# Experts' tokens gathered for two pairs at once in split products of 256 columns, the scatter moved to the pairs between, and the spare weight buffer removed

## What is computed

```python
# hier_moe: 32 experts in 4 groups of 8, top 2 within the chosen group
g_logits = h @ w_grp + b_grp; grp = argmax(g_logits)
top_val, top_idx = lax.top_k(e_logits of that group, 2)
gate = softmax(top_val) * p_grp
for each expert e, on its tokens xb:
    out = (silu(xb @ w1[e]) * (xb @ w3[e])) @ w2[e]
y = sum over a token's two experts of gate * out
x = x + g2 * y
```

## Time and profile before

| what | value |
|---|---|
| runs of the kernel before | 1750.25, 1750.30, 1751.11 us, median 1750.3 |
| profiled execution, its own time | 1750.12 us |
| its span | 1748.3 us |
| outside the span | 1.8 us |
| TensorE busy, share of the span | 99% |
| granted TensorE clock, mean | 0.998 |
| DMA, mean of the program | 244 GB/s |
| experts, first issue of a load to the end | 1258.2 to 1748.3 us |

### The profile page before, as it was taken

How to read it: one execution, slowest core, us unless ns; L and a number is a source line. 1 busy time by engine, 2 the same in 40 slices (tenths; PEclk the granted TensorE clock), 3 DMA queues, 4 the chain that set the end, 5 groups by cost and what they waited for, 6 DMA issues and landing times.

```text
span 1748.3 us, 30291 instructions
## 1 busy us (share of the span) xinstructions
PE 1729.7 (99%) x12581; PEld 1415.8 (81%) x12582; DVE 908.9 (52%) x1570; ACT 701.2 (40%) x1179; POOL 166.2 (10%) x173
## 2 busy tenths in 40 slices
PE   9999999999999999999999999999999999999998
PEld 8999988999999999998899999677774445444443
DVE  6655577676655766567678666466731111111111
ACT  6444545464344543454445445454631111111111
POOL 1000042210000100014214000100410000000000
PEclk9999999999999999999999999999999999999999
DMA  9545464545444445557556455232199999999997
GB/s 381 198 173 182 156 250 168 208 169 172 178 181 169 169 173 180 179 169 241 194 192 226 172 192 189 89 85 73 75 421 405 429 427 428 428 428 430 427 428 312
DMA packets 78815, 425.89 MB, mean 244 GB/s; under 512 B 16352, under 2 KB 32992, under 8 KB 41824
## 3 DMA queue, kind: packets, MB, share of 16 engines
q1 hardware_dynamic: 78256, 421.01, 62.7%
q10 hardware_dynamic: 432, 3.10, 0.4%
HBM read 423.03 MB, written 1.05 MB: 243 GB/s over the span
## 4 chain that ended last, share of the span: by engine, by line
PE 90%; DMA 6%; ACT 2%; DVE 2%; issue 1%; POOL 0%; POOLq 0%; SPq 0%; DVEq 0%; ACTq 0%
PE ps L721 18%; PE ps L723 18%; PE ps L722 18%; PE ps L1373 10%; PE ps L1424 5%; DMA ring<-stream_expert 5%; PE ps L1347 3%; PE ps L1049 2%; PE ps L1043 2%; PE ps L1055 2%; PE ps L815 1%; PE ps L1354 1%; ACT w_split L1486 1%; PE ps L1355 1%; DVE w_split L1939 1%
## 5 line engine op out<-in xcount | busy, mean ns | idle before, releaser
L1939 DVE TENSOR_TENSOR w_split<-ring,w_split 128x1024 fp32r<-128x1024 f32 x335 | 425.0, 1276 | 334.1 <-ACT w_split L1486 333.5
L721 PE MATMUL ps<-x_hi,w_split 128*128 128x272 f32 (+1 forms) x1856 | 541.1, 292 | 2.1 <-DVE x_lo L1944 1.7
L723 PE MATMUL ps<-x_hi,w_split 128*128 128x272 f32 (+1 forms) x1856 | 534.0, 288 | 0.0
L722 PE MATMUL ps<-x_lo,w_split 128*128 128x272 f32 (+1 forms) x1856 | 532.1, 287 | 0.0
L1486 ACT ACTIVATE w_split<-ring 128x1024 fp32r<-128x1024 f32 x335 | 350.6, 1054 | 354.4 <-PE ps L723 353.2
L721 PEld LDWEIGHTS ps<-x_hi,w_split 128*128 128x128 f32 x1856 | 350.4, 189 | 14.6 <-issue 9.6
L722 PEld LDWEIGHTS ps<-x_lo,w_split 128*128 128x128 f32 x1856 | 350.4, 189 | 0.3
L723 PEld LDWEIGHTS ps<-x_hi,w_split 128*128 128x128 f32 x1856 | 350.3, 189 | 0.0
L723 PE MATMUL ps<-hid_hi,w_split 128*128 128x272 f32 (+1 forms) x704 | 201.6, 286 | 0.0
L722 PE MATMUL ps<-hid_lo,w_split 128*128 128x272 f32 (+1 forms) x704 | 201.5, 286 | 0.0
L721 PE MATMUL ps<-hid_hi,w_split 128*128 128x272 f32 (+1 forms) x704 | 201.1, 286 | 0.0
(11 more groups left out here) (427 smaller groups left out, 2212.5 us busy)
## 6 DMA issues: line engine op xcount, KB each, us to landing
ring<-stream_ffn SPq DMA_DIRECT2D x131, 1024.0 KB, 4.8
ring<-stream_expert SPq DMA_DIRECT2D x48, 2048.0 KB, 25.0
ring<-stream_expert SPq DMA_DIRECT2D x36, 1024.0 KB, 12.8
arena<-stream_expert SPq DMA_DIRECT2D x16, 2048.0 KB, 25.5
ring<-stream_in SPq DMA_DIRECT2D x27, 1024.0 KB, 4.9
ring<-stream_mod SPq DMA_DIRECT2D x24, 1024.0 KB, 6.9
con<-stream_expert SPq DMA_DIRECT2D x8, 2048.0 KB, 26.1
ring<-stream_out SPq DMA_DIRECT2D x12, 1024.0 KB, 4.9
```

The lines of the kernel that those rows point to most:

```text
L721: pe.matmul(to, w[:, 0, k], hi, start=first, stop=False)
L722: pe.matmul(to, w[:, 0, k], lo, start=False, stop=False)
L723: return pe.matmul(to, w[:, 1, k], hi, start=False, stop=last_)
L1939: nc.vector.tensor_tensor(w[:, 1], half_of(n), w[:, 0].bitcast(fp32), ALU.subtract).then_inc(split_ready, 1)
```

## The change

- **Gather.** After pair 0 tokens are no longer gathered for each pair. In pairs 1, 3, ... 13 (`own == 1`) TensorE gathers the tokens of the next two pairs at once (`gather_two`): 256 columns, and the transposed features split into a high and a low float32r part (`h2t_hi`, `h2t_lo`), 32 products in all: 16 between gate and up, 8 on each side of the four transposes. Pairs 0 and 1 are still gathered one by one in float32 (`gather_one`). The selection `sel` becomes float32r and twice as wide.
- **Split.** In pair 0 ScalarE copies `h2t` to `h2t_hi` (two of 128x1024) and VectorE subtracts (two of 128x1024) into `h2t_lo`, which lies over `h2t`.
- **Scatter.** In pairs 2, 4, ... 14 the scatter of the pair before is done after up, four blocks on each side of the four transposes; in the other pairs up to 13 it stays between gate and up. In pair 15 nothing moves.
- **Tokens.** `xs` now holds two pairs' tokens in three pieces (`token_chunks`). The scaling is of 256 columns, four blocks on ScalarE and four on VectorE in every second pair. `e_hid` is gone: the product goes into `e_act` in place. `sel_gate` moves to the table memory.
- **No spare.** The memory of the spare is now `h2t_hi` and the last tokens (the tensor `vec` grows by 512 columns). `place_of` is gone: half q of unit m goes to the place of unit m-9, and waits for exactly that half (`again`). `whole` waits for the second half of unit m-9.
- **Loop.** Two iterations of six pairs in place of four of three, on TensorE, ScalarE and VectorE. SyncE's loop is as before.

```diff
-            for (unit, q), freed in zip(units(RING_SLOTS, 2 * RING_SLOTS), [None] + units(0, RING_SLOTS)):
...
-                    if freed is not None:
-                        sp.wait_ge(big_done, pass_ * PASS_DONE + big_used(*freed))
...
+                for unit, q in units(RING_SLOTS, 2 * RING_SLOTS):
+                    again(pass_, 0, unit, q)
                 for unit in range(2 * RING_SLOTS):
...
-                    whole(pass_, 1, unit, unit >= RING_SLOTS)
+                    whole(pass_, 1, unit)
```

```diff
+            def gather_two(n, bank, first):
+
+                pe.wait_ge(sel_ready, n + 3)
+                for c in (first, first + 1):
+                    to = ps[:, bank, (c % 2) * SEQ:(c % 2) * SEQ + SEQ]
                     for t in range(2):
...
+                        pe.matmul(to, h2t_hi[:, t, c * P:c * P + P], sel[:, t], start=t == 0, stop=False)
+                        last = pe.matmul(to, h2t_lo[:, t, c * P:c * P + P], sel[:, t], start=False, stop=t == 1)
                 last.then_inc(gathered, 1)
```

```diff
+                first = isinstance(i, int) and i == 0 and u == 0
+                two = own == 1 and more_pairs
...
+                gate_or_up(pass_, i, u, 0, halves, own)
+                if first or two:
+                    pe.wait_ge(selT_ready, n + 1)
+                    pe.wait_ge(ye_ready, 2 * n + 2)
+                    scatters(range(C))
+                if two:
+                    if isinstance(i, int) and i == 0 and isinstance(pass_, int):
+                        pe.wait_ge(split_ready, H2_DONE)
+                    gather_two(n, 6, 0)
+                    gather_two(n, 7, 2)
+                gate_or_up(pass_, i, u, 1, halves, own)
+                if first:
+                    gather_one(n + 1, 0, 1, tokens_of(pass_))
+                elif two:
+                    pe.wait_ge(xs_ready, n + 2)
+                    gather_two(n, 6, 4)
                 else:
...
+                    pe.wait_ge(ye_ready, 2 * n + 2)
+                    scatters(range(C // 2))
                 pe.wait_ge(e_hid_ready, n + 1)
```

```diff
+                if own == 1 and more_pairs:
+                    act.wait_ge(big_done, n * (2 * BIG_SLOTS) + 6)
+                    gathered_two(n, 0)
+                    gathered_two(n, 1)
+                if first:
+                    if split:
+                        for t in range(2):
+                            last = nc.scalar.activation(h2t_hi[:, t], h2t[:, t], ACT.Copy)
+                        last.then_inc(hi_ready, 1)
+                    gathered_one(n + 1, 1)
```

More of the change, by code:

```diff
@@ L646, in again, with whole @@
                 big(i * TURN + u, u, b, q)
-            def whole(pass_, i, unit, wait):
-                if wait:
-                    sp.wait_ge(big_done, pass_ * PASS_DONE + i * TURN_DONE + big_used(unit - RING_SLOTS, 1))
+            def whole(pass_, i, unit):
+                sp.wait_ge(big_done, pass_ * PASS_DONE + i * TURN_DONE + big_used(unit - RING_SLOTS, 1))
                 u, b = divmod(unit, BIG_SLOTS)
@@ L1372, in gate_or_up, with pair @@
                             w = first_half(u, 2 * part + e, q, 4, FE)[:, c % 4] if first else big_slot(u, 2 * part + e, C, FE)[:, c]
-                            last = pe.matmul(ps[rows, 4 + part, 0:FE], xs[:, c, rows], w, start=c == 0, stop=c == C - 1)
+                            last = pe.matmul(ps[rows, 4 + part, 0:FE], token_chunks(c)[:, own, rows], w, start=c == 0, stop=c == C - 1)
                             if c % 4 == 3:
                                 last.then_inc(big_done, 1)
-            def pair(pass_, i, u, halves, more_pairs=True):
+            def pair(pass_, i, u, halves, own, more_pairs=True):
@@ L1395, in pair @@
                 last.then_inc(pair_turned, 1)
-                if more_pairs:
-                    gather(n + 1, 1)
-                else:
-                    for o in range(C // 2, C):
-                        scatter(o, False)
+                if first:
+                    gather_one(n + 1, 1, 1, tokens_of(pass_))
+                elif two:
+                    pe.wait_ge(xs_rest_ready, n + 2)
+                    gather_two(n, 7, 6)
+                else:
+                    scatters(range(C // 2, C))
@@ L2639, in pair @@
+            def pair(n, expert, own, more_pairs=True, first=False, split=False):
+                two = own == 1 and more_pairs
                 dve.drain()
                 dve.wait_ge(pair_turned, 2 * n)
-                nc.vector.tensor_tensor(sel_gate, sel, by_slot(R["gate"], expert), ALU.mult).then_inc(sel_gate_ready, 1)
+                nc.vector.tensor_tensor(sel_gate, slots(own, 1).bitcast(fp32), by_slot(R["gate"], expert, 2), ALU.mult).then_inc(sel_gate_ready, 1)
                 dve.drain()
-                if more_pairs:
-                    select(expert + 1)
+                if first:
+                    select(expert + 1, 1, 1)
+                if two:
+                    select(expert + 1, 0, 2)
+                    dve.wait_ge(big_done, n * (2 * BIG_SLOTS) + 6)
+                    gathered_two(n, 0)
@@ L2645, in pair @@
                 dve.wait_ge(e_act_ready, n + 1)
                 dve.wait_ge(big_done, n * (2 * BIG_SLOTS) + 8)
-                nc.vector.tensor_tensor(e_hid, e_act, ps[:, 5, 0:FE], ALU.mult).then_inc(e_hid_ready, 1)
-                if more_pairs:
-                    gathered_tokens(n + 1)
+                nc.vector.tensor_tensor(e_act, e_act, ps[:, 5, 0:FE], ALU.mult).then_inc(e_hid_ready, 1)
+                if two:
+                    gathered_two(n, 1)
+                if first:
+                    gathered_one(n + 1, 1)
+                    if split:
+                        dve.wait_ge(hi_ready, H2_DONE)
+                        for t in range(2):
+                            last = nc.vector.tensor_tensor(h2t_lo[:, t], h2t[:, t], h2t_hi[:, t].bitcast(fp32), ALU.subtract)
+                        last.then_inc(split_ready, 1)
```

196 lines of the change are left out of this document (99 added, 97 removed).

## The result

| | before | changed |
|---|---|---|
| median of 20 runs each | 1750.71 us (1749.81 to 1752.86) | 1753.01 us (1751.85 to 1754.51) |
| profiled execution | 1750.12 us | 1752.8 us |
| its span | 1748.3 us | 1751.0 us |
| up's second half in the last pair starts | 1726.55 us | 1729.07 us |

The ratio is 1.0014, with a 95% interval of 1.0007 to 1.002. The change costs 2.3 us. That is within the 0.2% that I had called no change, but it is a real loss, and 0.4 us above my range.

The account below looks back on a forecast made before the run. The weight stream was taken as the bound, 29.4 us a pair at 428 GB/s. Profiled 1750.12 - 0.15 (stops) + 0.2 (code) = 1750.2 us; with the median 0.2 us above the profiled execution, forecast 1750.3 us, range 1748.3 to 1752.6 us.

Parts of the forecast that it names:

- the one on code: Longer loop's extra code fetched beside the weight stream: 0.07 to 0.21 MB, 0.2 to 0.5 us, taken as 0.2 us.
- TensorE's saving: Gathering two pairs at once takes 4.2 us, not 7.54; seven such pairs save 23.4 us of TensorE, nothing at the end.
- The waits: TensorE's waits for loads in the experts' stage were to grow to about 30 us.
- The stops: Weight stream in pairs 0 and 1: new stops of 0.36 and 1.49 us replace 2.0 us near 1350 us, gaining 0.15.
- The first, a stream dry again and again: Stream stands 1.47 us at each of four counts in pair 0: 1756 us, chance 0.08.
- The second: Clock falls in TensorE's longer waits from the seventh pair; counts only behind the last wait: 1752.0 us, chance 0.07.
- a sign that the prediction is wrong: A granted clock under 1.00 between 1480 and 1740 us in the experts' stage would show the forecast wrong.
- The third: No stop at all: loads issued into a moving queue start sooner than 1.47 us, the 1.85 us vanish: 1748.4 us, chance 0.08.
- fourth: Faster weight stream, 431 GB/s held over 340 us, 2.4 us less; without the load stops too, 1746 us; chance 0.03.
- the fifth: Split gather no cheaper than before, so TensorE saves nothing: still 1750.3 us, chance 0.02.
- My other sign: A weight stream ending later than 1736 us would show the forecast wrong.
- That TensorE does not stop for its code: In the stage's loop, TensorE was not to stop for code fetches, as in the earlier trace's window at the same load.

Follow-up runs that it names:

- the kernels with 21 packets: Kernel before with six-pair loop on TensorE, ScalarE and VectorE: 1754.4 us; that plus new load order without spare: 1753.35 us; six-pair loop on TensorE alone: 1754.27 us.
- the order alone: Kernel before, without the spare and with the changed kernel's order and waits of loads, loop and gather as before: 1750.31 us, ratio 0.9998.
- the kernel with less code: Changed kernel without the second expert's products and the scatter in the loop's twelve pairs (output lacks them): 1749.99 us, ratio 0.9994.

## Why the prediction was wrong

**The failed step is the one on code**, "0.07 to 0.21 MB, 0.2 to 0.5 us at 428 GB/s. I take 0.2 us". The amount was nearly right: 20 - 8 = 12 packets more, 0.2 MB, since the second turn does fetch all six pairs again, the case that I had only called possible. The price was wrong. I divided bytes by the rate of all sixteen engines, as if a packet were shared among them. Each sits on one engine for 1.0 us, only eight engines carry them, and the last load waits for the slowest engine. The term measured 2.3 us here and 2.7 to 3.7 us in the kernels with 21 packets, more than ten times what I took. I had not bounded its price from rows on both sides: the earlier trace rows also hold the time on one engine, 1.0 us a packet, and twelve of these on one engine would have been 12 us as the upper end. A range with even a third of that would have held the result.

**What held.** TensorE's saving was worth nothing. Sixteen split products of the new gather took from 1334.97 to 1336.86 us, 0.12 us each against my 0.131, so two pairs save 3.7 us, and none of it arrived. A pair took 25.7 us (gate of pair 3 at 1377.23 us, of pair 5 at 1428.63) against my 25.8. TensorE had caught up at pair 7, as I had said (7 or 8). The waits were 20.8 us instead of about 30, and part of the difference is in products that ran slower. The stops, 0.36 + 1.49 us for 2.00, gave equal bytes up to 1360 us, and the order alone measured -0.4 us with an interval (about 1.6 us either way) that holds my -0.15 and much else. No wait of TensorE on the split shows in pairs 0 and 1.

**The rivals.** The first, a stream dry again and again, did not happen: 422 GB/s from 1262 to 1304 us and no dent there. The second happened without its price. The clock fell to 0.83 in several windows, which I had listed as a sign that the prediction is wrong; it is none, because the waits absorb 1.8 us of slower gate as long as the last pair is spared, and the kernel with less code, which waits longest, is at 1749.99 us. The Trainium skill (TensorE: Matmul & The Clock Gate, section HAM oscillation) warns of this. The trace agrees that the clock falls (0.83), and not that it costs anything where the stream sets the end. The third and fourth did not occur, and the fifth is refuted by the 0.12 us. My other sign did its work: I had named a stream end later than 1736 us, and it came at about 1738.

That TensorE does not stop for its code was right but for one place, the jump back of the longer loop (0.8 us in the changed kernel, 2.1 to 2.8 us in the three others), which the row of before could not show. The Trainium skill (Runtime: NRT & Kernel Launch, Instruction fetch mechanics) calls the cost of crossing a block of 16 KiB mostly hidden, and gives TensorE 128 KiB for its code. The traces fit the second: three pairs are four packets, 64 KB, and stay; six pairs are about eight and are fetched again. With the first they agree for TensorE's time within a turn, and not for the DMA engines': in this stage, which they bound, a block costs 0.2 to 0.3 us.

## What to carry to other kernels

Where the weights' stream sets the end, count the code packets of a stage beside its bytes, and keep TensorE's loop short enough to stay loaded; a faster TensorE buys nothing there, and its longer loop costs. A load ends with its slowest DMA engine, so price whatever sits on a single engine (code, a one-row load) by its time on that engine, not by its bytes over all sixteen, and read the busy share in the last windows of a stream to see whether the engines end together. Here code went round eight of the sixteen engines, so count what the fullest of the eight gets.

## What was unexpected of the hardware

- A loop of three pairs (four packets of code in the stretch 1360 to 1700 us) stays loaded; one of six is fetched anew each turn. Code for ScalarE and VectorE in a loop twice as long added one packet of 8 KB there, and no time.
- A packet of code holds its DMA engine for 1.0 to 1.1 us, weights of the same 16 KB for 0.62 us. The packets go round eight engines of sixteen.
- At the jump back of a loop of six pairs TensorE stopped for 0.8 to 2.8 us; at that of a loop of three pairs, whose code was not fetched again, it did not.
- 24 single-row loads of 8 KB, 0.2 MB beside the 145 MB of this stretch, cost 6.2 us; the same bytes in 16 rows a load 1.5 us, a loss that the runs can't tell from none.
- The granted clock fell to 0.83 and gate took 8.8 instead of 7.02 us in two pairs of the chain, at no cost to the end.
- Ending 1 to 2 us of the stream earlier for most engines moved the last load's landing by nothing in one of two profiles.
